# Eighteen groups of idle matrix products with other shapes and reading orders, ahead of a two-block transformer's first weights

## What is computed

```python
for l in range(DEPTH):                      # first block
    h = _rms_norm(x, attn_norm[l]) @ w_in[l]
    ...
    x = x + mix @ w_o[l]
    gate, up = jnp.split(_rms_norm(x, ffn_norm[l]) @ w_gate_up[l], 2, axis=-1)
    x = x + (jax.nn.silu(gate) * up) @ w_down[l]
```

## Time and profile before

| what | us |
|---|---|
| median of 3 runs | 1678.62 |
| lowest, highest | 1677.86, 1681.99 |
| the profiled execution, its own time | 1683.09 |
| its span, first to last instruction | 1681.3 |
| TensorE busy in the span | 1641.5 (98%) |
| TensorE's weight loads | 1585.0 (94%) |
| VectorE busy | 1202.8 (72%) |
| ScalarE busy | 900.3 (54%) |
| GpSimd busy | 113.7 (7%) |
| DMA, read from memory | 271.13 MB, 162 GB/s over the span |

### The profile page before, as it was taken

How to read it: one execution, slowest core, us unless ns; L and a number is a source line. 1 busy time by engine, 2 the same in 40 slices (tenths; PEclk the granted TensorE clock), 3 DMA queues, 4 the chain that set the end, 5 groups by cost and what they waited for, 6 DMA issues and landing times.

```text
span 1681.3 us, 31825 instructions
## 1 busy us (share of the span) xinstructions
PE 1641.5 (98%) x13566; PEld 1585.0 (94%) x13566; DVE 1202.8 (72%) x1765; ACT 900.3 (54%) x1378; POOL 113.7 (7%) x72
## 2 busy tenths in 40 slices
PE   9989999999999999999999999999999999999997
PEld 9978999999789999989999989999999999999997
DVE  5887777556977776477858768983677768679863
ACT  5585644454675444544545665544445446655542
POOL 2020000020110000210000110001200001110000
PEclk9999999999999999999999999999999999999999
DMA  8313555553225555555335435554454345345550
GB/s 294 109 59 114 196 197 189 173 194 126 95 86 183 202 201 182 211 203 189 114 134 189 136 125 195 198 193 165 165 197 162 132 155 184 120 151 207 197 184 34
DMA packets 53406, 275.03 MB, mean 164 GB/s; under 512 B 6288, under 2 KB 6928, under 8 KB 53136
## 3 DMA queue, kind: packets, MB, share of 16 engines
q1 hardware_dynamic: 52544, 271.15, 46.3%
q10 hardware_dynamic: 720, 1.84, 0.3%
HBM read 271.13 MB, written 1.05 MB: 162 GB/s over the span
## 4 chain that ended last, share of the span: by engine, by line
PE 75%; DVE 16%; ACT 5%; issue 2%; POOL 1%; DMA 0%; ACTq 0%; SPq 0%; DVEq 0%; POOLq 0%
PE bank L787 16%; PE bank L789 15%; PE bank L790 15%; DVE weights_lo L652 4%; PE scores L787 3%; PE scores L789 3%; PE scores L790 3%; PE heads L787 2%; PE heads L790 2%; PE heads L789 2%; ACT weights_hi L641 1%; DVE x_lo L934 1%; PE scores L1915 1%; ACT probs L1205 1%; PE heads L1943 1%
## 5 line engine op out<-in xcount | busy, mean ns | idle before, releaser
L652 DVE TENSOR_TENSOR weights_lo<-raw,weights_hi 128x1536 fp32r<-128x1536 f32 (+2 forms) x344 | 583.8, 1716 | 226.8 <-ACT weights_hi L641 226.4
L641 ACT ACTIVATE weights_hi<-raw 128x1536 fp32r<-128x1536 f32 (+4 forms) x352 | 499.9, 1440 | 179.5 <-PE bank L790 82.7
L787 PE MATMUL bank<-x_hi,weights_lo 128*128 128x256 f32 (+1 forms) x1588 | 443.7, 279 | 2.5 <-DVE weights_lo L652 2.1
L789 PE MATMUL bank<-x_lo,weights_hi 128*128 128x256 f32 (+1 forms) x1588 | 440.3, 277 | 0.0
L790 PE MATMUL bank<-x_hi,weights_hi 128*128 128x256 f32 (+1 forms) x1588 | 440.3, 277 | 0.0
L787 PEld LDWEIGHTS bank<-x_hi,weights_lo 128*128 128x128 f32 (+1 forms) x1588 | 297.4, 187 | 6.5 <-DVE weights_lo L652 2.8
L789 PEld LDWEIGHTS bank<-x_lo,weights_hi 128*128 128x128 f32 (+1 forms) x1588 | 296.9, 187 | 0.1
L790 PEld LDWEIGHTS bank<-x_hi,weights_hi 128*128 128x128 f32 (+1 forms) x1588 | 296.5, 187 | 0.0
L787 PE MATMUL bank<-hidden_hi,weights_lo 128*128 128x256 f32 x692 | 191.5, 277 | 0.4 <-DVE hidden_lo L2254 0.4
L789 PE MATMUL bank<-hidden_lo,weights_hi 128*128 128x256 f32 x692 | 191.1, 276 | 0.0
L790 PE MATMUL bank<-hidden_hi,weights_hi 128*128 128x256 f32 x692 | 191.1, 276 | 0.0
(11 more groups left out here) (427 smaller groups left out, 3427.4 us busy)
## 6 DMA issues: line engine op xcount, KB each, us to landing
raw<-in_w_b SPq DMA_DIRECT2D x194, 768.0 KB, 4.2
raw<-in_w_a SPq DMA_DIRECT2D x120, 768.0 KB, 4.2
raw<-in_w_a SPq DMA_DIRECT2D x16, 512.0 KB, 3.4
raw<-in_w_b SPq DMA_DIRECT2D x10, 512.0 KB, 4.0
raw<-in_w_b SPq DMA_DIRECT2D x2, 752.0 KB, 4.5
raw<-in_w_a SPq DMA_DIRECT2D x2, 736.0 KB, 8.2
raw<-in_w_b SPq DMA_DIRECT2D x2, 720.0 KB, 5.0
raw<-in_w_a SPq DMA_DIRECT2D x2, 672.0 KB, 6.9
```

Of the source, the lines that this page charges most:

```text
L641: nc.scalar.activation(whi[c % SPLIT][:, 0:n], raw[c % RAW][:, 0:n], ACT.Copy).then_inc(*s.mark("weights_hi", c))
L652: nc.vector.tensor_tensor(wlo[c % SPLIT][:, 0:n], raw[c % RAW][:, 0:n], whi[c % SPLIT][:, 0:n].bitcast(F32), ALU.subtract).then_inc(*s.mar ...
L787: ins = nc.tensor.matmul(dst, wl, xh, start=start, stop=False, skip_group_check=skip)
L789: nc.tensor.matmul(dst, wh, xl, start=False, stop=False, skip_group_check=skip)
```

## The change

`keep_busy` ahead of `cq0` now issues 4 products instead of 44. Behind them a new function `reads` issues 18 kinds of products, 5 of each, 90 in all. Their operands come from a new tile `PROBE` (`idle_rows`, 128 x 1024, float32r, at the place of `probs_t`), which VectorE fills with zeros by a cast from `QUIET`. The cast stands between VectorE's first memset and the other two, and waits for a new first part of the mark `eps`; what TensorE, ScalarE and GpSimd wait for is still set by the last memset, which is now behind the cast. The kinds differ in:

- the stationary operand: 64 columns (`few`); 128 columns at column 512 (`high`), at 520 (`half_on`), at 528 (`line_on`); or 128 columns with a step of 2;
- the number of moving columns: 256, 512 or 2;
- the order in which the moving columns are read: as they lie; `turns(ap, a)`, column 0 of each of `a` parts, then column 1 of each, and so on, so that two columns read one after the other lie 32 to 256 apart; `blocks(ap, j)`, which takes turns between two halves in runs of `j` columns.

Of the 90 products 20 read 256 columns as they lie or in blocks, 35 read 256 in turns, 10 read 512 in turns, and 25 read 2 columns. Nothing reads what they write.

```diff
--- before.py
+++ after.py
@@ -513,6 +513,7 @@
         ML = a1.place("mix_lo", (10, T), F32R)
         GR = place("rope_gain_rows", (2, NR), F32, a1.at)
         PA = [a1.place(f"probs{i}", (QT, T)) for i in range(2)]
+        PROBE = place("idle_rows", 2 * PAIR, F32R, a1.at)
         PTA = [a1.place("probs_t", (QT, T)), two(PART[:, :])]
 
         a2 = Area(after_tables)
@@ -712,6 +713,31 @@
             for _ in range(n):
                 nc.tensor.matmul(ps[:, T:T + P], QUIET[:, 0:1].to_broadcast([P, P]), QUIET[:, 0:1].to_broadcast([P, P]), start=True, stop=True, skip_group_check=True)
 
+        def reads(ps):
+
+            def row(o, n):
+                return PROBE[:, o:o + n]
+
+            def turns(ap, a):
+                return ap.rearrange("p (a n) -> p n a", a=a)
+
+            def blocks(ap, j):
+                return ap.rearrange("p (a n j) -> p n a j", a=2, j=j)
+
+            low, few = row(0, T), row(PAIR, P // 2)
+            high, half_on, line_on = row(PAIR, P), row(PAIR + 8, P), row(PAIR + 16, P)
+            out = ps[:, 0:T]
+            for stationary, moving, dst in (
+                    (few, low, out), (few, turns(low, 2), out), (few, turns(low, 4), out), (few, turns(low, 8), out),
+                    (few, blocks(low, 16), out), (few, blocks(low, 8), out), (few, turns(row(0, PAIR), 2), ps[:, :]), (high, turns(row(0, PAIR), 2), ps[:, :]),
+                    (few, row(0, 2), ps[:, 0:2]), (high, row(0, 2), ps[:, 0:2]), (half_on, row(0, 2), ps[:, 0:2]), (line_on, row(0, 2), ps[:, 0:2]),
+                    (PROBE[:, PAIR:PAIR + 2 * P:2], row(0, 2), ps[:, 0:2]),
+                    (high, turns(low, 2), out), (high, turns(low, 4), out), (half_on, turns(low, 2), out),
+                    (high, turns(row(4, T), 2), out), (high, low, out)):
+                m = math.prod(stationary.shape[1:])
+                for _ in range(5):
+                    nc.tensor.matmul(dst[0:m], stationary, moving, start=True, stop=True, skip_group_check=True)
+
         WAITS = {"p1_sum": 3, "p1_factor": 3, "p2_sum": 7, "p2_factor": 3, "ua0": 7, "p3_sum": 7, "p3_factor": 3, "q0": 7}
 
         def first_products(pl, pe, l, name, hi_ready):
@@ -721,7 +747,8 @@
             keep_busy(ps, WAITS.get(name, 0) if name != "q0" or l else 0)
             if name == "cq0" and l == 0:
                 pe.wait_ge(*O.at(0, "eps"))
-                keep_busy(ps, 44)
+                keep_busy(ps, 4)
+                reads(ps)
             hi, lo, ready = pl.operands[job.operand]
             steps = [(t, k) + job.tiles[t][k][1:] for t in range(len(job.tiles)) for k in range(KD)]
             by_rows = sorted(steps, key=lambda step: step[1]) if name in ROWS_FIRST else steps
@@ -2682,7 +2709,9 @@
 
         @block.vector
         def _(dve):
-            nc.vector.memset(QUIET[:, :], 0.0)
+            nc.vector.memset(QUIET[:, :], 0.0).then_inc(*O.mark("eps", "rows"))
+            dve.wait_ge(*O.at(0, "eps", "rows"))
+            nc.vector.tensor_copy(PROBE[:, :], QUIET[:, 0:1].to_broadcast([P, 2 * PAIR]))
             nc.vector.memset(HALF[:, :], -0.5)
             nc.vector.memset(eps_col, EPS).then_inc(*O.mark("eps"))
```

## The result

The median of 18 runs is **1682.11 us** (1679.83 to 1685.37); the kernel before, on the same chip, had 1678.59 us (18 runs, 1676.28 to 1682.23). The ratio, estimated from all these runs, is 1.0019, 95% interval [1.0011, 1.0026]: 3.2 us slower (1.8 to 4.4; the two medians lie 3.5 us apart), where +9.2 was forecast. That is within half a microsecond of the first rival's time (1681.7). The profiled execution took 1682.08 us on a span of 1680.3. The order of operations, waits and engines is as it was; `L713` is now `L714`, `L737` `L764`, `L740` `L767`, `L787` `L814`, `L652` `L653`, and the new products are `L739`.

A forecast was written before the change was run, and what follows sets the result against it. TensorE, busy 98% of the span, was taken as the bound. The first real product at 3.8 + 16.9 + 1.0 + 1.0 = 22.7 us, 9.5 late, gave +9.2 after the pause: 1678.6 + 9.2 = 1687.8 us, range 1681.5 to 1700.

The forecast's parts named there:

- the first rival: Same 45 new products: the interleaved orders cost nothing, so not measurably slower, 1681.7 us; chance 0.2.
- The path: TensorE's head: everything added before the first real product delays all behind it, except about 0.25 us of slack.
- The interleaved orders: New products with columns read 32 elements or more apart: 0.22 us per 256 columns, 0.44 per 512, 12.1 us together.
- The other product terms: Remaining new products: contiguous and blocks 2.3 us, 2 columns on 128 stationary 2.2 us, on 64 stationary 0.3 us.
- The start: VectorE's cast (1.0 us) and a new wait (0.1) make TensorE start at 2.1 us instead of 0.98.
- The clock: Over the new products: +1.0 us for work at 1.2 GHz at first, +1.0 us for a possible later return to it.
- the rise: TensorE goes from 1.2 to 2.4 GHz 5 us after its first product, at 7.1 us.
- The fall: The clock may drop back to 1.2 GHz with the 2-column products: once in two times, +1.0 us, from 0 to 4.
- What moves behind: First real product at 22.7 instead of 13.2; all later work, waits at 80 to 150 us included, moves along: +9.2 us.
- The pause: TensorE's wait for `weights_lo` of chunk 2 before the first L787 product, 0.25 us, was to disappear.

The follow-up runs named there:

- the bursts: Spacing-only looks: bursts of 20 fp32r products, one reading order each, behind 44 idle products; 0.120 us as they lie, 0.112 turns of 2, 0.222 turns of 8.
- experiment 12: The changed kernel itself, unedited, timed again beside fresh runs of the kernel before: 1681.62 us for 1678.79, ratio 1.0014.
- experiment 1: The changed kernel with every moving operand of the new products read as it lies, same counts and shapes: 1684.76 us for 1680.49 before, ratio 1.0025.
- experiment 2: The changed kernel without its 25 products of 2 columns: 1682.34 us for 1680.49 of the kernel before, ratio 1.0007.
- experiment 8: The changed kernel with its 25 products of 2 columns moved ahead of the other 65: 1687.49 us for 1681.7 of the kernel before, ratio 1.0033.
- Experiment 3: The kernel before with 66 plain idle products instead of 44: 1684.8 us for 1680.49, ratio 1.0031.
- experiment 10: Kernel before with x2, x3, merged, h stored even tokens first, token-major weights even columns first, both read in turns of 2: 1666.63 us for 1680.48, 0.9911.

## Why the prediction was wrong

The path was right and the size wrong, and one term did it.

- **"The interleaved orders ... 35 x 0.22 + 10 x 0.44 = 12.1 us": this step failed.** By the bursts, and experiment 12 for turns of 4, the 45 products cost at 2.4 GHz: turns of 2, 5 x 0.109 + 15 x 0.112 = 2.2; turns of 4, 5 x 0.143 + 5 x 0.143 = 1.4; turns of 8, 5 x 0.220 = 1.1; 512 columns, 10 x 0.216 = 2.2. Together that is 6.9 us, 5.2 less than forecast, and only 0.5 more than the estimate for the same products as they lie (experiment 1). The reason given, that fp32r reads a new element with almost every tick and has no room for an order that brings one useful element per fetch, is refuted by turns of 2 at 0.112 us. 0.22 us is right only for turns of 8 (5 of the 45) and nearly so for single streams of step 2 or 4 (0.227 and 0.233), which the change doesn't have. (The pass that the 0.22 was read from works out at (1.97 - 0.39)/7 = 0.226 us, a slip of 0.3 us in the sum.)
- *The other product terms.* Contiguous and blocks: 2.3 forecast, 5 x (0.113 + 0.120 + 0.120 + 0.124) = 2.4 measured. 2 columns: 0.112 and 0.058 us, as taken; the stationary with step 2 cost 0.118, near its lower end. The sum of all is 11.9 us for 16.9.
- *The start* was 0.4 us too late, by the cast (0.69 for 1.0).
- *The clock.* The stretch at 1.2 GHz before the rise was worth 1.0 us in experiment 12, as forecast: nine products at 0.213 instead of 0.11. The fall, which I gave one chance in two, is in one profile of this kernel and not in the other. Of the 1.94 us between 16.40 and 18.34, the fall makes 1.47 and the rise, 1.9 us later, only 0.47: it met turns of 4, 0.07 us dearer at 1.2 GHz, and turns of 8, which take 0.220 us at either clock. Experiments 1, 2 and 8 suggest that the clock's behaviour hangs on the products of 2 columns; with one profile each, and a fall that comes in some executions only, they don't show it.
- *Check of the sum:* 3.41 + 11.9 + 1.0 = 16.3, measured 16.40.
- *What moves behind:* right. The pause went, the waits from 80 to 156 us kept their lengths, and the delay of 4.4 us at 31 us was still there at 270. Experiment 3 turned 4.8 us of delay at the first L787 product into 5.2 us (3.0 to 7.2).
- **The first rival** had 16.5 us for the first real product, 1681.7 us without a fall and up to 1684.8 with one, and decided at 0.15 us per unit of 256 columns. Measured were 6.9 / 55 = 0.126 us, 16.40 or 18.34, and 1682.11 and 1681.62. The expected +2.9 to +4.8 from the two starts of the first L814 product brackets the +3.2. It came this close in part by luck: the products were 0.8 us dearer than it had them, and the start 0.4 and the stretch at 1.2 GHz 0.6 us cheaper. And "cost nothing" is right only for the sum; turns of 8 and 4 cost more than contiguous reads, turns of 2 and 512 columns less.
- *The two rules of the Trainium skill.* "SBUF — State Buffer", in its note on cachelines, has each read of a new line of 16 bytes pay. For turns of 8 (0.222 us) the trace agrees. For turns of 2, where every column is in another line than the one before, it disagrees: 0.112 us is the fastest of all. Every 2nd column, with two hits per line, should be free by it and cost 0.227. The sentence of "TensorE: Matmul & The Clock Gate", "The mechanism", that a weight load overlaps a product only on other rows of the array is contradicted here as in the trace before: 20 products on 128 stationary columns came every 0.112 us, each with its load. The same section of the Trainium skill also lets a load be pulled ahead into a background weight buffer, which the prediction left out and with which these spacings agree.

I weighed the interleaved price by an argument on fetches where the nearest row was silent, and passed over what the trace before did show: that contiguous products came at 0.113 in one stretch and at 0.118 us in another with nothing waited for. That suggests that reading was already part of the price, and that an order could move it either way.

## What to carry to other kernels

- When a price can't be bounded more closely than by a factor of two or four, its middle is no forecast: with ends of 0.113 and 0.44 us the honest likeliest result was as open as the ends, and the free case deserved more than 0.2.
- On a kernel bound by back-to-back fp32r products, look at their spacing against the best seen. Reading the moving operand as two streams in turns, 4 or more columns apart, took 0.113 to 0.120 us to 0.112 and, done for most of the products, the whole kernel down by 0.9% (0.7 to 1.1, experiment 10), at the price of storing even and odd columns apart. Not in pairs, not in eight streams, and not as one stream with a step: these cost 0.167, 0.222 and 0.227 us.
- In this kernel no wait between 31 and 270 us swallowed any of the delay. The likely reason, which no run here tests, is that none of them ended on something that runs by itself.
- Here the clock's falls differ between executions of one program and shift everything behind them by 1 to 2 us. For effects of a few microseconds, read the delay at one and the same product and take the total from many runs.

## What the runs showed of the hardware

- A 256-column fp32r product on 128 stationary columns came, at 2.4 GHz, every 0.112 us (turns of 2; also one column repeated), 0.113 or 0.118 to 0.120 us (as it lies, two paces; in bursts it moved with the start of the read), 0.122 to 0.125 (blocks of 8), 0.129 (blocks of 4), 0.135 to 0.144 (turns of 4), 0.167 (pairs), 0.222 (turns of 8) and 0.227 to 0.233 (step 2 and 4). 512 columns came every 0.216 us in turns of 2, every 0.224 to 0.236 as they lie and every 0.333 in pairs. The price doesn't simply fall with the length of a contiguous piece, and none of the runs shows why; a theory of this order remains open.
- Writing an output bank in pairs costs nothing (0.120 us with and without). Single columns in turns were not tried for the output.
- At 1.2 GHz contiguous products and turns of 2 and 4 all came every 0.213 us, so these orders are free there. Turns of 8 came every 0.220 us at 1.2 GHz and every 0.220 to 0.222 at 2.4: their price didn't change with the granted clock.
- Whether the granted clock falls behind a run of 2-column products differs between executions of one program (the changed kernel at 14.24 us in one profile, not at all before 148 us in the other).
